# A norm moved behind its projections: factors applied to the outputs at the border of two transformer blocks

## The reference

```python
def first_block(x, ...):
    ...
    x = x + hierarchical_moe(h, ...)
    return rmsnorm(x, final_g)

def rms_norm(x, w):
    y = x * lax.rsqrt(jnp.mean(x * x, axis=-1, keepdims=True) + EPS)
    return y * w

def second_block(x, p, w_in, ...):
    h = x
    u = rms_norm(h, norm_pre_mix)
    proj = u @ w_in
    hq, hf, hi, hg, nq, nkv, ngate, ga, gb = jnp.split(proj, SPLIT_POINTS, axis=-1)
    ...  # hgrn2_mixer(hq, hf, hi, hg), nsa_mixer(nq, nkv, ngate), gates ga, gb
    h = h + rms_norm(merged @ w_out, norm_post_mix)
    ...
```

## Time and profile before

| | us |
|---|---|
| median of 3 runs | 1365.38 (1364.94 to 1366.89) |
| the profiled execution | 1364.1 |
| its span, first to last instruction | 1362.3 |
| TensorE busy (matmuls) | 1157.6, 85% |
| VectorE busy | 655.0, 48% |
| ScalarE busy | 426.0, 31% |
| mean granted TensorE clock | 0.923 |

### The profile page before, as it was taken

How to read it: one execution, slowest core, us unless ns; L and a number is a source line. 1 busy time by engine, 2 the same in 40 slices (tenths; PEclk the granted TensorE clock), 3 DMA queues, 4 the chain that set the end, 5 groups by cost and what they waited for, 6 DMA issues and landing times.

```text
span 1362.3 us, 17066 instructions
## 1 busy us (share of the span) xinstructions
PE 1157.6 (85%) x7324; PEld 858.1 (63%) x7324; DVE 655.0 (48%) x1027; ACT 426.0 (31%) x605; POOL 9.2 (1%) x19
## 2 busy tenths in 40 slices
PE   6999999997576566666667999999999999999987
PEld 6977889742121212212116988888888989998865
DVE  3799855621010000101004488885678865664473
ACT  2353634210000000000002456542476614553442
POOL 0000000000000000000000000000000000000000
PEclk9997999988897888888778999999989999999998
DMA  8533285499999999999991543444434044555420
GB/s 352 186 132 116 81 357 187 170 385 429 427 426 429 426 427 430 427 427 430 427 427 60 170 153 128 155 133 142 186 132 179 16 177 172 186 186 185 162 116 31
DMA packets 26862, 332.62 MB, mean 244 GB/s; under 512 B 3120, under 2 KB 3392, under 8 KB 4896
## 3 DMA queue, kind: packets, MB, share of 16 engines
q1 hardware_dynamic: 25760, 328.47, 60.7%
q0 software_dynamic: 1024, 3.02, 0.7%
HBM read 330.43 MB, written 1.05 MB: 243 GB/s over the span
## 4 chain that ended last, share of the span: by engine, by line
PE 56%; DMA 29%; DVE 11%; ACT 2%; issue 2%; SPq 0%; DVEq 0%; ACTq 0%
DMA ring<-in_w_up 10%; PE ps L544 10%; PE ps L563 9%; PE ps L616 9%; DMA ring<-in_w_gate 7%; PE ps L648 6%; PE ps L1162 6%; DMA arena<-in_w_up 3%; DMA ring<-in_w_down 3%; DMA arena<-in_w_down 3%; PE ps L879 2%; DMA ring<-in_units 2%; PE ps L990 2%; DVE parts L1295 2%; DVE arena L1355 2%
## 5 line engine op out<-in xcount | busy, mean ns | idle before, releaser
L1295 DVE TENSOR_TENSOR parts<-ring,parts 128x2048 fp32r<-128x2048 f32 x68 | 155.3, 2292 | 122.6 <-ACT parts L2027 122.2
L563 PE MATMUL ps<-parts 128*128 128x512 f32 x768 | 180.3, 394 | 0.0
L2027 ACT CAST parts<-ring 128x2048 fp32r<-128x2048 f32 x68 | 129.5, 1909 | 155.8 <-PE ps L544 63.0
L544 PE MATMUL ps<-parts 128*128 128x256 f32 x1344 | 164.8, 285 | 3.0 <-DVE parts L1295 3.0
L544 PEld LDWEIGHTS ps<-parts 128*128 128x128 f32 x1344 | 163.4, 193 | 3.6 <-DVE parts L1295 2.1
L563 PEld LDWEIGHTS ps<-parts 128*128 128x128 f32 x768 | 144.8, 190 | 30.8 <-issue 1.1
L879 PE MATMUL ps<-ring,arena 128*32 128x512 f32 x640 | 100.6, 763 | 63.0 <-DMA ring<-in_w_gate 36.8
L1604 DVE TENSOR_TENSOR arena<-arena,ps 128x512 f32<-128x512 f32 x32 | 22.0, 688 | 255.5 <-PE ps L916 255.4
L616 PE MATMUL ps<-parts 128*128 128x512 f32 x576 | 137.9, 399 | 5.1 <-DVE parts L1311 4.7
L616 PEld LDWEIGHTS ps<-parts 128*128 128x128 f32 x576 | 109.6, 192 | 28.4 <-DVE parts L1311 5.0
L879 PEld LDWEIGHTS ps<-ring,arena 128*32 128x32 f32 x640 | 20.5, 125 | 138.6 <-issue 54.2
(11 more groups left out here) (332 smaller groups left out, 1310.1 us busy)
## 6 DMA issues: line engine op xcount, KB each, us to landing
ring<-in_units SPq DMA_DIRECT2D x38, 2048.0 KB, 8.2
ring<-in_w_gate SPq DMA_DIRECT2D x20, 2048.0 KB, 45.5
ring<-in_w_up SPq DMA_DIRECT2D x20, 2048.0 KB, 45.2
ring<-in_w_down SPq DMA_DIRECT2D x17, 2048.0 KB, 45.7
ring<-in_units SPq DMA_DIRECT2D x31, 1024.0 KB, 5.1
arena<-in_w_down SPq DMA_DIRECT2D x12, 2048.0 KB, 45.3
arena<-in_w_gate SPq DMA_DIRECT2D x10, 2048.0 KB, 44.8
arena<-in_w_up SPq DMA_DIRECT2D x8, 2048.0 KB, 46.2
```

The costliest lines, as they stand in the source:

```text
L544: mm = nc.tensor.matmul(banks[f][:, half * T:half * T + T], w[:, k, at:at + P], v[:, 4 * h + k, :], start=h + half + k + n == 0, stop=h + ...
L563: mm = nc.tensor.matmul(banks[t], v[:, 4 * h + k, t * P:t * P + P], w[:, k, :], start=h + k + n == 0, stop=h == 1 and k == 3 and n == 2)
L1295: step(V.tensor_tensor(rest_half(name, h), split_half(name, h), w_high[stage][h].bitcast(F32), ALU.subtract), f"{stage}_rest_ready", wait= ...
L2027: step(S.copy(w_high[stage][h], split_half(name, h)), f"{stage}_high_ready", wait=False)
```

## The change

x itself is turned, not the normed x, and the two norms are applied around the product.

- Turns: TensorE turns all of x at once (16 transposes), by feature halves. ACT writes the high part straight from PSUM with final_g * norm_pre_mix (`gain_pre`, one column a block of 128 features) as its scale; DVE writes the rest by one `scalar_tensor_tensor` per block.
- hq0 and hq1 become split products too. hq0 has an order of its own (`first_projection`): high by high of both halves, then high weight by rest of x, then rest weight by high. hq0 now goes to slot 0 and hq1 to slot 1; hf0 follows hq0 in slot 0. ACT casts hq0's high halves before the branch.
- Factors: ACT squares x with running sums (`squares`), the first factor is applied to x on DVE (x with final_g is still needed for the residual), the second sums are taken of that, and `factor` is the product of both. For the feature-major outputs hq and hf it must lie along the free axis: two plain products of ones by a diagonal spread it over all partitions in the middle of hf0 (`spread_factor`), ACT copies it out, and DVE multiplies each bank (`scaled`). The token-major outputs get it as the scale of the copy that ACT made before.
- Block 2's small gate product (48 columns) still reads xT in float32: GpSimd adds high and rest into xT.

```diff
+        factor_diag, factor_row = page(9, 0, 256), page(9, 1664, 256)
-                slot = (2, 1)[m] if m < 2 else m % 2 if m < 17 else LATE_SLOTS[m - 17] if m < 25 else (2, 0, 1, 6)[(m - 25) % 4]
+                slot = m % 2 if m < 17 else LATE_SLOTS[m - 17] if m < 25 else (2, 0, 1, 6)[(m - 25) % 4]
@@ TensorE
-                normed_half("mix2T", 0, 5)
-                half_turned("mix2T", 0)
-                feature_pair(["hq0", "hq1"], xT, lambda: normed_half("mix2T", 1, 6), lambda: half_turned("mix2T", 1))
-                pe.wait_ge(sem("proj_x_rest_ready"), 1)
-                for c in range(2):
-                    split_feature_major(f"hf{c}", f"hf{c}", proj_high, proj_rest)
+                for f in range(2):
+                    for t in range(TT):
+                        bank = open_bank(f"mix2T{t}{f}")
+                        for j in range(4):
+                            k = 4 * f + j
+                            mm = nc.tensor.transpose(bank[:, j * P:j * P + P], x[:, t, k * P:k * P + P], ident)
+                        close_bank(mm, f"mix2T{t}{f}")
...
+                    for h in range(2):
+                        pe.wait_ge(sem("proj_high_ready"), h + 1)
+                        pe.wait_ge(sem("turned_high_ready"), turned_count["mix2T"] + 2 * h + 2)
+                        product(0, h, w_high["proj"][h], proj_high)
+                    for h in range(2):
+                        drained_by(pe, f"mix2T0{h}", f"mix2T1{h}")
+                        product(1, h, w_high["proj"][h], proj_rest).then_inc(sem("first_high_used" if h else "proj_half_used"), 1)
+                    for h in range(2):
+                        pe.wait_ge(sem("proj_rest_ready"), h + 1)
+                        product(2, h, rest_half(name, h), proj_high)
...
+                first_projection("hq0")
+                split_feature_major("hq1", "hq1", proj_high, proj_rest)
+                split_feature_major("hf0", "hf0", proj_high, proj_rest, spread_factor)
+                split_feature_major("hf1", "hf1", proj_high, proj_rest)
@@ VectorE
+                for f in range(2):
+                    for t in range(TT):
+                        bank = filled_by(dve, f"mix2T{t}{f}")
+                        dve.wait_ge(sem("turned_high_ready"), turned_count["mix2T"] + 2 * f + t + 1)
+                        for j in range(4):
+                            k = 4 * f + j
+                            ins = V.scalar_tensor_tensor(out=proj_rest[:, k, half_of(t)], in0=bank[:, j * P:j * P + P], scalar=gain_pre[:, k:k + 1],
+                                                         in1=proj_high[:, k, half_of(t)].bitcast(F32), op0=ALU.mult, op1=ALU.subtract)
+                        drain(ins, f"mix2T{t}{f}")
+                for h in range(2):
+                    split_rest("proj", 0, h)
+                dve.wait_ge(sem("raw_sums"), TT)
+                step(V.tensor_scalar(inv_raw, sums_raw, 1.0 / D, EPS, ALU.mult, ALU.add), "variance_ready", wait=False)
+                for h in range(2):
+                    split_rest("proj", 1, h)
+                inverse_root(inv_raw)
...
-                    scaled_norm(x, x[:, t, :], 40, t, gain_final, normed[:, t, :])
-                    if t:
-                        half_turned("mix2T", xT, 0, "norm_pre_mix_2")
-                    normalize_half(x, normed, 44, t)
-                half_turned("mix2T", xT, 1, "norm_pre_mix_2")
...
+                def scaled(fill, dst):
+                    bank = filled_by(dve, fill)
+                    ins = V.tensor_tensor(grid(dst, 2), grid(bank, 2), wide(factor_row.unsqueeze(1), [P, 2, T]), ALU.mult)
+                    drain(ins, fill, wait=True)
@@ ScalarE
+                act.wait_ge(sem("moe_piece_used"), SIDE * (last_piece_in(("slot", 2)) + 1))
+                for h in range(2):
+                    split_high("proj", 0, h)
...
+                            ins = S.activation(proj_high[:, k, half_of(t)], bank[:, j * P:j * P + P], ACT.Copy, scale=gain_pre[:, k:k + 1])
+                        step(ins, "turned_high_ready", wait=False)
+
+                def squares(sums):
+                    for t in range(TT):
+                        ins = S.activation(page(8, 1024 * t, 1024), x[:, t, :], ACT.Square, accum_out=sums[:, t:t + 1])
+                        step(ins, "raw_sums", wait=t == TT - 1)
+
+                squares(sums_raw)
+                for h in range(2):
+                    split_high("proj", 1, h)
+                root()
+                split_high("proj", 2, 0)
+                act.wait_ge(sem("x_final"), TT)
+                squares(sums_final)
+                root()
@@ GpSimd
                 pool.dma_start(gain_final, d["final_g"].partition_broadcast(P)).then_inc(sem("final_gain_landed"), 16)
+                drained_by(pool, *[f"mix2T{t}{f}" for t in range(TT) for f in range(2)])
+                nc.gpsimd.tensor_tensor(xT, proj_high.bitcast(F32), proj_rest.bitcast(F32), ALU.add).then_inc(sem("xT_ready"), 1)
@@ SyncE
-                for n in range(n_early, n_early + 3):
-                    last_piece = max(m for m in range(PIECES * QUADS) if expert_places[m % n_places] == ("slot", units[n][2]))
-                    sp.wait_ge(sem("moe_piece_used"), SIDE * (last_piece + 1))
+                for n in range(n_early, n_early + 2):
+                    sp.wait_ge(sem("moe_piece_used"), SIDE * (last_piece_in(("slot", units[n][2])) + 1))
                     load(n)
```

More of the change, by code:

```diff
@@ L402, in expert_landed, with last_piece_in @@
             return sem(f"{tag}_landed{m % places_of[tag]}"), 0
+        def last_piece_in(place):
+            return max(m for m in range(PIECES * QUADS) if expert_places[m % places_of["moe"]] == place)
         sum_banks = [5, 6, 0, 7]
@@ L2452, in _ @@
                     load_more_experts()
-                for n in range(n_early + 3, len(units)):
+                for n in range(n_early + 2, len(units)):
                     load(n)
```

154 lines of the change are left out of this document (99 added, 55 removed).

## The result

The changed kernel took 1357.11 us (median of 4 runs, 1354.38 to 1358.77) beside 1366.14 us for the kernel before (4 runs, 1364.94 to 1367.57): a ratio of 0.9944, 95% interval 0.9932 to 0.9956. It is faster, by 6.0 to 9.3 us, where 11.9 were forecast; the time lies inside the stated range of 1350.8 to 1358.0, near its upper end.

What follows compares the result with a forecast made beforehand. TensorE was taken as the bound after the expert stage, held at the border by DVE's norms. Gain 14.1, less 0.5 hand-overs and 1.7 clock, is 11.9 us: 1352.2 profiled, 1353.5 median, range 1350.8 to 1358.0.

Steps and rivals of the forecast that it cites:

- three signs named for being wrong: First products wait past 722, hf0's first half lands after 741, or gaps at hf0, hf1, hi0 sum over 2 us.
- The forecast's 13.6 with no clock fall: Gain from last expert product to hf1's end: 14.1 us less 0.5 for hand-overs, before any clock loss.
- the start: Behind the expert stage: TensorE's transposes begin at 718.03, 1.21 us after the last drain; 7.0 us gained from the start.
- the turns: From first transpose at 718.03 to first product at 720.9: four transposes, a hand-over and two banks copied by ACT.
- the 2.2 allowed for clock and hand-overs: Deducted on the stretch to hf1's end: 0.5 us for some ten engine hand-overs, 1.7 for the clock.
- A: Main case: clock falls near 721 and is back 3.4 us after products begin; 1353.5 us, chance 0.35.
- the 1.7 us: Clock loss at the first products: 3.4 us at half speed cost 1.7 us.
- B: The clock holds through the transposes at the border, nothing lost: gain 13.6, time 1351.8 us, chance 0.22.
- Rival C: GpSimd's xT addition blocks DVE's rests: 0, 1.0 or 3.3 us lost, 2.2 taken; 1354.0 or 1355.7 us, chance 0.26.
- In both kernels by the same steps, so what the stretch gains is passed on: Behind hf1: hi0 and the forget gates follow as before, so the whole gain reaches the end.
- D: DVE becomes the bound from 718 to 768, rests slip; 4 to 8 us of gain left, 1359 us, chance 0.09.
- E: Slower than before: late halves of hq1 to hi0 stop TensorE, 4.2 us each; 1368.5 us, chance 0.05.

Runs made afterwards that it cites:

- e1: Changed kernel with GpSimd's addition that rebuilds xT waiting for x with the first factor instead of the turned banks; 1352.75 us, ratio 0.9926.
- e5: Changed kernel with TensorE's wait for the last sums behind the branch and GpSimd's addition later; 1350.49 us, ratio 0.9904.
- e6: e5 with TensorE's load of the count also moved ahead of the expert stage; 1349.97 us, ratio 0.9895.
- e10: e6 with ACT's two waits ahead of the forget gates' logarithm also exchanged; 1350.4 us, ratio 0.9897.
- e2: Changed kernel with the jumped-over loop for further experts replaced by one wait on TensorE alone; 1352.5 us, ratio 0.992.
- e11: Changed kernel with TensorE's jumped-over loop cut to 58 products and transposes instead of 122; 1353.36 us, ratio 0.9925.
- e12: Changed kernel with TensorE's jumped-over loop lengthened to 228 products and transposes instead of 122; 1357.04 us, ratio 0.9948.
- e8: Kernel before, with the jumped-over loop for further experts left out on TensorE; 1364.64 us, ratio 1.0.
- e3: Changed kernel with TensorE's wait for the last expert sums moved behind the branch; 1353.4 us, ratio 0.993.
- e4: Changed kernel with TensorE's load of the count moved ahead of the expert stage; 1355.59 us, ratio 0.9935.
- e9: Changed kernel with ACT's waits for factor and gates, ahead of the forget gates' logarithm, exchanged; 1353.18 us, ratio 0.9932.
- e7: Changed kernel with both norms back ahead of the turns and the output factors set to one, split products kept; 1366.33 us, ratio 1.001.

## Why the prediction was right and where it was wrong

The mechanism was right. The norms left TensorE's path, the products ran as split ones at 0.121 to 0.124 us each at the high clock (17.51 for 144, 11.88 for 96), four units ran without a break from hq1 on, and hf0's load, which now comes late, cost nothing: issued at 739.78, cast at 747.43, with no wait on TensorE, although its first half took 7.65 us to land and not 4.9 to 5.1. That it is issued together with the second half accounts for a part only: where GpSimd's addition comes later (e1, e5, e6, e10), and with it the small loads that GpSimd issues behind it, it is 5.8 us; where they fall together it is 7.65 to 9.9. Of the three signs named for being wrong two were seen (the first products waited past 722, this half landed after 741), the third, gaps of over 2 us in sum at hf0, hf1 and hi0, was not. The forecast's 13.6 with no clock fall was even reached: e5 and e10 take 51.5 from 66.0 (14.5).

The forecast of 11.9 failed, and the step that failed is the start: "TensorE has the same load of the count and the same branch, so I let its 16 transposes begin at 718.03." VectorE's 1.21 us was taken for an engine whose jumped-over loop is much longer in instructions. It took 4.64 us, 3.4 more than the step says. Of the table's 4.3 us between forecast and measurement the start is 3.5, hq0 with the wait behind it 2.5 and the turns 0.6, less the 2.2 allowed for clock and hand-overs. e2 shows it (1.18 us without the loop), e11 and e12 show that it depends on the loop's length by a step, the packets of instructions show what comes with that step, and e8 shows why it couldn't be read from a row of before. A bound from below and above, as the other unknown costs had, would have shown it: the wait of 7.85 us in the earlier trace rows was all that limited TensorE's own way from above.

The clock went as in A, and the 1.7 us look near: 0.6 from the transposes to the first product and 1.0 at hq0 (12.90 against 11.9). But the 1.0 cost nothing, since hq0 and the wait behind it take 14.4 us at either clock; that the two sums agree is luck. It also went otherwise than I gave. It fell at 722.6, when TensorE had been idle since 718.0 and no transpose had run; and it was back 2.6 us after the first product, where 3.4 were assumed. Where the start was early (e2, e5, e6, e10, e11) it didn't fall, as in B, though by e3 and e4 transposes alone don't hold it; why it held stays open. The Trainium skill, "TensorE: Matmul & The Clock Gate", Part 4, says that transposes don't count as work for the clock. That it fell amid them in e3 and e4 agrees; that it rose in e9 while nothing but transposes had run since 722.16 doesn't, and there the measurement decides.

Rival C came true as well, next to A: forecast nothing, 1.0 or 3.3 us, measured 1.54 here, 2.54 where hq0 ran at the high clock (e2). The price of this rival is the 2.54, as hq0 at the low clock hid 1.0 of it. Its mechanism was as told, but the instruction it stopped wasn't one of the rests: it was a scaling of 128x2 elements behind them, which has no two SBUF inputs. The addition alone takes 4.62 us (e1): the upper bound, twice the nearest row of 2.29, was right, the middle was not. The 4497 ns of the Trainium skill, "GPSIMD Engine Reference", 3.1, were close. The lock told by the Trainium skill, "SBUF — State Buffer", summary and port table, agrees: the rests ran at 2.24 us each with GpSimd waiting, and then VectorE waited. That page of the Trainium skill names, beside two inputs, a two-port performance mode of VectorE; whether the small scaling was in one no run shows.

"In both kernels by the same steps, so what the stretch gains is passed on" failed too: 2.63 us were given back at the second level. The diff adds a wait for the factor ahead of the logarithm, at no cost by itself, and it moved the load of the table behind the gates. TensorE loses 0.5 us by it at hi1's start and 1.0 at the wait before the level; in e9 0.1 of these 1.5 are left. The rest is the clock, which was low for more of the second level (6.46 us against 5.30).

D and E did not happen: no wait above 0.5 us between hq1 and the second level, and no second one of the kind in a row.

Not forecast, and in the other direction: the clock falls later in the program. From the end of hi1's level on, this pair differs by 3.4 us at pauses of equal length. In the profiled executions that part took 546.8 to 547.1 us in before and e8, 546.7 in e7, 546.8 in e3, 546.2 in e1, and 543.0 to 544.3 in the other nine. These are single executions, one of each kernel. By them most kernels with the change took some 3 us less there, which would account for most of what lies between the 5.0 us of the border (7.65 less 2.63) and the 9.0 of the medians; how often each kernel does so isn't known. So it is in part luck that the time lies inside the range: with the border's 5.0 us alone it would have been 1360.4, above it. What decides at which pause the clock falls stays open.

## What to carry to other kernels

When an engine is moved to the front of a path, read its own way to that point anew: an instruction stream behind a long loop that is jumped over may start microseconds later than its neighbour's, and it stays invisible as long as another engine is later. Put waits behind such a branch rather than ahead of it, so that the way runs beside the work waited for. Keep GpSimd's large element-wise work out of any span in which VectorE is on the path, even by tiny instructions, and where ACT must switch its table before a waiting instruction, let the wait that is fulfilled early stand last of two, checking in the trace which instruction carries the late one.

## What the runs showed of the hardware

- TensorE's way past a loop that isn't entered: 1.2 to 1.3 us with one wait or 58 products in it, 4.3 to 4.8 us with 122 or 228. The long way comes with one 16 KB packet on the queue of instructions, 2.3 to 2.8 us ahead of the first transpose, in all nine runs that have it, and with none in e2 and e11. With the wait for the sums behind the branch it is partly hidden (1.03 us in e5, 2.6 in e3).
- The granted clock fell to 0.50 while 16 transposes ran (e3, at 717.1), rose to 1.00 while only such transposes ran (e9, at 725.4), and stayed at 1.00 where the split products began at 722.37 after the last expert product's end at 717.62 (e5).
- GpSimd's addition of two 128x2048 fp32 tiles takes 4.62 us alone, and a VectorE instruction of 128x2 elements stands while it runs: 4.63 instead of 0.17 us.
- ACT's table load took 1.28 us in every kernel, and whether it hides in a wait depended on which of two waits stood on it (e9).
- The first half of hf0 (1 MB) took 7.65 us from its issue to its cast, with the second half and small loads of GpSimd under way at the same time; the DMA engines were 87% busy and moved 262 GB/s, 1.64 MB for SyncE and 0.38 MB for GpSimd, and the latter took 26.7% of the engines' time. With GpSimd's loads later it took 5.8 us (e1, e5, e6, e10).
